# Sample state products by head, on four row groups of TensorE in two rounds of four

## The reference, cut to what matters

```python
b_last = b[:, :, -1:, :]
S_new = jnp.exp(b_last[:, :, 0, :, None]) * S + jnp.einsum(
    'bhsk,bhsv->bhkv', kc * jnp.exp(b_last - b), vc)
```

## Time and profile before

| what | value |
|---|---|
| median of 3 runs | 2166.18 us (2164.0 to 2167.3) |
| the profiled execution, its own time | 2165.37 us |
| its span, first to last instruction | 2163.8 us |
| mean granted TensorE clock | 0.972 |
| PE busy (matmul) | 2046.5 us, 95% |
| DVE busy | 1569.3 us, 73% |
| ACT busy | 1287.0 us, 59% |
| POOL busy | 769.2 us, 36% |

### The profile page before, as it was taken

The page is one execution under the profiler, slowest core; times in us unless marked ns, Lnnn a source line. Parts: engine busy times, 40 slices in busy tenths (PEclk is TensorE's granted clock), DMA queues, the critical chain, the costliest instruction groups (busy, mean ns, idle before and its releaser), DMA issues.

```text
span 2163.8 us, 38715 instructions
## 1 busy us (share of the span) xinstructions
PE 2046.5 (95%) x11913; PEld 1499.0 (69%) x11947; DVE 1569.3 (73%) x2132; ACT 1287.0 (59%) x1717; POOL 769.2 (36%) x997
## 2 busy tenths in 40 slices
PE   6998999999968999999999999999999999999994
PEld 4896676666646676676676668877676677788562
DVE  4533456666668687787786769988797798898657
ACT  3532344333416676676775667867676786888554
POOL 3225345555723232222242223432243243334124
PEclk8999999999968999999999999999999999999997
DMA  9767611121367788898887779999899899999765
GB/s 348 231 226 256 189 50 49 52 70 46 97 221 296 275 315 291 290 338 310 294 306 243 281 270 382 390 339 365 288 366 347 289 349 333 366 370 392 258 221 182
DMA packets 154531, 572.26 MB, mean 264 GB/s; under 512 B 22560, under 2 KB 41773, under 8 KB 120165
## 3 DMA queue, kind: packets, MB, share of 16 engines
q1 hardware_dynamic: 127405, 511.87, 62.7%
q0 software_dynamic: 25520, 56.53, 10.5%
q10 hardware_dynamic: 1552, 3.13, 0.4%
HBM read 521.36 MB, written 50.29 MB: 264 GB/s over the span
## 4 chain that ended last, share of the span: by engine, by line
PE 58%; issue 4%; ACT 4%; DVE 3%; ACTq 0%; DVEq 0%; DMA 0%; POOLq 0%
PE pg L2242 9%; PE pg L2243 9%; PE pg L2245 9%; PE py L2201 6%; PE py L2177 6%; PE py L2178 5%; PE py L2181 5%; PE pg L2215 3%; ACT hi L2378 3%; PE pt L2172 1%; PE pt L2166 1%; DVE lo L2475 1%; PE pg L2235 1%; PE pt L2187 0%; ACT L2398 0%
## 5 line engine op out<-in xcount | busy, mean ns | idle before, releaser
L2242 PE MATMUL pg<-hi,xs 128*128 128x512 f32 x1056 | 432.9, 410 | 0.0
L2243 PE MATMUL pg<-lo,xs 128*128 128x512 f32 x1056 | 412.5, 391 | 0.0
L2475 DVE TENSOR_TENSOR lo<-spare,hi 128x1024 fp32r<-128x1024 f32 x264 | 306.3, 1221 | 81.5 <-ACT hi L2378 78.6
L2475 DVE TENSOR_TENSOR lo<-w_out,hi 128x1024 fp32r<-128x1024 f32 x272 | 313.8, 1220 | 70.4 <-ACT hi L2378 69.3
L2245 PE MATMUL pg<-hi,xs 128*128 128x512 f32 x1056 | 326.1, 390 | 0.0
L2475 DVE TENSOR_TENSOR lo<-raw,hi 128x1024 fp32r<-128x1024 f32 x264 | 314.0, 1220 | 7.1
L2378 ACT ACTIVATE hi<-w_out 128x1024 fp32r<-128x1024 f32 x272 | 265.5, 1049 | 34.6 <-SPq L2009 27.2
L2378 ACT ACTIVATE hi<-spare 128x1024 fp32r<-128x1024 f32 x264 | 259.2, 1048 | 43.2 <-PE pg L2245 43.2
L2378 ACT ACTIVATE hi<-raw 128x1024 fp32r<-128x1024 f32 x264 | 270.4, 1056 | 23.3 <-PE pg L2245 23.3
L2242 PEld LDWEIGHTS pg<-hi,xs 128*128 128x128 f32 x1056 | 198.5, 188 | 71.6 <-issue 14.1
L2245 PEld LDWEIGHTS pg<-hi,xs 128*128 128x128 f32 x1056 | 198.5, 188 | 42.5
(11 more groups left out here) (486 smaller groups left out, 3571.2 us busy)
## 6 DMA issues: line engine op xcount, KB each, us to landing
w_out<-in_w_gu SPq DMA_DIRECT2D x136, 1024.0 KB, 6.9
spare<-in_w_gu SPq DMA_DIRECT2D x132, 1024.0 KB, 10.2
raw<-in_w_down SPq DMA_DIRECT2D x132, 1024.0 KB
ada_w<-in_w_ada SPq DMA_DIRECT2D x4, 2048.0 KB
spare<-in_w_ada SPq DMA_DIRECT2D x4, 2048.0 KB
moe_rows<-small SPq DMA_DIRECT2D x9, 512.0 KB, 7.0
w_v<-in_w_in SPq DMA_DIRECT2D x2, 2048.0 KB, 17.2
w_i<-in_w_in SPq DMA_DIRECT2D x2, 2048.0 KB
```

The costliest lines, as they stand in the source:

```text
L2242: pe.matmul(pg[u][b][:, :], xs[:, kt, 0, :], wh[:, u, :], start=False, stop=False)
L2243: pe.matmul(pg[u][b][:, :], xs[:, kt, 0, :], wl[:, u, :], start=False, stop=False)
L2475: dve.tensor_tensor(lo[q % RING][:, :, :], grain(q % GRAINS), hi[q % RING][:, :, :].bitcast(F32), ALU.subtract).then_inc(s["lo"], 1)
```

## The change

The same products are laid out by head. The keys of the four heads stand in four groups of 32 partitions (`kT` is now 128 x 128), and so do the values (`v4`, and `Vz` with all heads, 128 partitions by 128 values for each sequence). A matmul takes the 32 rows of one head and streams four sequences at once (512 columns), into a bank of its own: X1, X2, X0 and L0 for the heads 0 to 3. There are two rounds of four matmuls. VectorE adds by head and half of the sequences, eight adds of 128 x 4 x 128. The keys reach their place by four matmuls with the identity (`columns_k_sample`) where there were four transposes, ScalarE copies the values once more (into `v4`), and VectorE copies the sequence mask into the three other groups near the program's start.

```diff
         sample = {**quarters(1, 0, ("f", "q", "k", "lf")), **quarters(1, 1, ("b", "eb", "dk", "kend")),
-                  **quarters(1, 2, ("lev0", "lev1", "A", "wd")), **quarters(1, 7, ("row0",)),
-                  "v": strip(1, 3), "gs": strip(1, 4), "o": strip(1, 5), "kT": strip(1, 6), "mixT": w_v[:, 7, 0:KT * NS],
+                  **quarters(1, 2, ("lev0", "lev1", "A", "wd")), **quarters(1, 7, ("row0", "v4")),
+                  "v": strip(1, 3), "gs": strip(1, 4), "o": strip(1, 5), "kT": strip(1, 6)[:, 0:P], "mixT": w_v[:, 7, 0:KT * NS],
...
-        Vz = w_g[0:NS, :, :]
+        Vz = w_g[:, 0:2, :].rearrange("p a (b v) -> p (a b) v", v=P)
...
-        state_ps = (X1, X2, X0, X1, X2, X0, X1, X2)
+        state_ps = (X1, X2, X0, L0)
+        ROUND = NB // 2
...
             for j in range(NB):
-                sp.wait_ge(s["S_s"], j + 1)
+                sp.wait_ge(s["S_s"], (j // ROUND + 1) * H)
                 sp.dma_start(out["S_s"][0, j].rearrange("h k v -> k h v"), S0[:, j, :, :]).then_inc(s["st_out"], 16)
...
-            def states_sample(t, first, end):
-                pe.wait_ge(s["kT"], t + 1)
-                pe.wait_ge(s["Vz"], 1)
-                for j in range(first, end):
-                    bank = state_ps[j]
-                    if j >= 3:
-                        pe.wait_ge(s["S_s"], j - 2)
-                    for m in range(H):
-                        last = pe.matmul(bank[:, m * P:(m + 1) * P], sample["kT"][0:NS, m * P:(m + 1) * P], Vz[:, j, m * P:(m + 1) * P], start=True, stop=True)
-                    last.then_inc(s["S_s_mm"], 1)
+            def columns_k_sample(t):
+                pe.wait_ge(s["kend"], t + 1)
+                for m in range(H):
+                    last = pe.matmul(X3[m * NS:(m + 1) * NS, 0:P], sample["kend"][:, m * NS:(m + 1) * NS], ident[:, :], start=True, stop=True)
+                last.then_inc(s["kT_ps"], 1)
+
+            def states_sample(t, half):
+                if half == 0:
+                    pe.wait_ge(s["kT"], t + 1)
+                    pe.wait_ge(s["Vz"], 1)
+                    pe.wait_ge(s["vrow"], 2)
+                    pe.wait_ge(s["x1"], TILES + 1)
+                else:
+                    pe.wait_ge(s["S_s"], H)
+                for m in range(H):
+                    rows_m = slice(m * NS, (m + 1) * NS)
+                    last = pe.matmul(state_ps[m][:, :], sample["kT"][rows_m, :], Vz[rows_m, half * ROUND:(half + 1) * ROUND, :], start=True, stop=True)
+                last.then_inc(s["S_s_mm"], 1)
...
-            transpose_k(u, NS, X3)
+            columns_k_sample(u)
...
-            states_sample(u, 0, 1)
             pe.wait_ge(s["lg"], t)
             route_rows(t, P)
-            pe.wait_ge(s["vrow"], 2)
-            states_sample(u, 1, 3)
+            states_sample(u, 0)
             route_logits(t, P)
             pe.wait_ge(s["lg"], u)
             route_rows(u, NS)
             pe.wait_ge(s["rank_used"], t)
             rank(t, P, X3)
             route_logits(u, NS)
-            states_sample(u, 3, 5)
             pe.wait_ge(s["rank_used"], u)
             rank(u, NS, X3)
-            states_sample(u, 5, NB)
+            states_sample(u, 1)
...
                 act.wait_ge(s["sam_mm"], 2)
+                act.activation(sample["v4"], X3[:, 0:P], ACT.Copy)
...
-                act.activation(of(T)["kT"][0:T, :], bank[0:T, :], ACT.Copy).then_inc(s["kT"], 1)
+                act.activation(of(T)["kT"][:, :], bank[:, :] if T == P else bank[:, 0:P], ACT.Copy).then_inc(s["kT"], 1)
...
-            def add_state(j):
-                dve.wait_ge(s["S_dec"], j + 1)
-                dve.wait_ge(s["S_s_mm"], j + 1)
-                rows = S0[:, j, :, :].rearrange("p h v -> p (h v)")
-                dve.tensor_tensor(rows, rows, state_ps[j][:, :], ALU.add).then_inc(s["S_s"], 1)
+            def add_state(half, m):
+                js = slice(half * ROUND, (half + 1) * ROUND)
+                dve.wait_ge(s["S_dec"], (half + 1) * ROUND)
+                dve.wait_ge(s["S_s_mm"], half + 1)
+                dve.tensor_tensor(S0[:, js, m, :], S0[:, js, m, :], state_ps[m][:, :].rearrange("p (j v) -> p j v", j=ROUND), ALU.add).then_inc(s["S_s"], 1)
...
+            for m in range(1, H):
+                dve.tensor_copy(seqmask[m * NS:(m + 1) * NS, :], seqmask[0:NS, :])
...
-            add_state(0)
+            add_state(0, 0)
             logits(t, P)
             choose(t, P)
             h2_high(u, T)
-            add_state(1)
+            add_state(0, 1)
             weigh(t, P)
             place(t, P, X3)
-            add_state(2)
+            add_state(0, 2)
             logits(u, T)
             choose(u, T)
-            for j in range(3, 6):
-                add_state(j)
+            add_state(0, 3)
             weigh(u, T)
             place(u, T, X3)
-            for j in range(6, NB):
-                add_state(j)
+            for m in range(H):
+                add_state(1, m)
...
+            pool.wait_ge(s["S"], 1)
             for j in range(NB):
-                last = pool.tensor_scalar(Vz[:, j, :], sample["v"][0:NS, :], seqmask[:, j:j + 1], 0.0, ALU.mult, ALU.add)
+                last = pool.tensor_scalar(Vz[:, j, :], sample["v4"], seqmask[:, j:j + 1], 0.0, ALU.mult, ALU.add)
```

More of the change, by code:

```diff
@@ L136, in mixing @@
         reset_s = sb("reset_s", [P, H * NS])
-        seqmask = sb("seqmask", [NS, NB])
+        seqmask = sb("seqmask", [P, NB])
         iota_e = sb("iota_e", [P, E])
@@ L1739, in _ @@
             pool.memset(reset_s[:, :], 1.0)
-            pool.memset(seqmask[:, :], 1.0)
+            pool.memset(seqmask[0:NS, :], 1.0)
             for m in masks:
@@ L1747, in _ @@
             pool.memset(reset_s[:, :].rearrange("p (g t) -> p g t", t=TS)[:, :, 0:1], 0.0)
-            pool.affine_select(out=seqmask[:, :], in_=seqmask[:, :], compare_op=ALU.is_ge, fill=0.0,
+            pool.affine_select(out=seqmask[0:NS, :], in_=seqmask[0:NS, :], compare_op=ALU.is_ge, fill=0.0,
                                base=0, pattern=[[-TS, NB]], channel_multiplier=1).then_inc(s["c0"], 1)
             pool.wait_ge(s["c0"], 5)
-            pool.affine_select(out=seqmask[:, :], in_=seqmask[:, :], compare_op=ALU.is_ge, fill=0.0,
+            pool.affine_select(out=seqmask[0:NS, :], in_=seqmask[0:NS, :], compare_op=ALU.is_ge, fill=0.0,
                                base=TS - 1, pattern=[[TS, NB]], channel_multiplier=-1)
```

## The result

The changed kernel took 2173.2 us (median of 8 runs, 2168.9 to 2175.3), the kernel before 2165.2 (8 runs, 2163.2 to 2167.3) in the same session: a ratio of 1.0035, 95% interval 1.0026 to 1.0044. That is 8 us slower, where 2166.0 and no measurable change were forecast, and outside the range.

A forecast was written before the change was run, and what follows sets the result against it. Bound: the barrier between `mixing` and `experts`, three arrivals within 1.0 us. Savings of 3.0 (listing) and 1.8 us (last add) end ahead of weights 0.6 later; barrier -0.2 on median 2166.18 gives 2166.0 us, range 2162.5 to 2170.0.

The forecast's parts named there:

- behind which everything starts anew: Barrier between `mixing` and `experts`: the change lies before it, so the barrier's line by instruction was read first.
- Rival 4: Clock or experts part shifts for reasons of its own, either sign, by up to 3.3 us; chance 0.07.
- Rounds: TensorE's four-matmul rounds: row groups run at once, 1.1 to 1.6 us, or 2.1 to 2.7 at the lower clock.
- Rival 3: TensorE's row groups don't run at once: second round 7.2 us, total 2171.0 to 2175.1 us; chance 0.07.
- First round: TensorE between tile 7's transposes and router logits: runs from 612.6 to 613.7 or 614.2, costing nothing.
- Logits: Tile 7's router logits behind the first round: end by 616.9, or 617.9 if the clock falls earlier, not holding VectorE.
- GpSimd's drain: Ahead of the barrier: starts 3.0 us earlier with the listing, over by 647.5 if it keeps its 7 us.
- rival 2: GpSimd's drain hangs on DMA traffic, not the listing: +0.6 to +0.8 us, 2166.8 to 2167.0; chance 0.18.
- Stores: Four state stores go out together at 633.05; weights behind them start 0.6 us later, bounds -0.5 and +0.8.
- the 0.6 of the sum: SyncE's end ahead of the barrier: 649.5 + 0.6 = 650.1 us, from weights going out later.
- the forecast of -0.2: The barrier opens at some 650.4 instead of 650.6 us; chance of the forecast 0.55.
- The 5.1 us for a first round one by one at the lower clock: Loss if the first round's row groups run one after the other at the lower clock; 1.0 at full clock.

The follow-up runs named there:

- e2: The kernel before with 166 idle TensorE instructions behind its last state product: 2176.9 us, 1.0053 of the kernel before.
- e1: The changed kernel with 90 idle TensorE instructions behind its last state product: 2165.2 us, 1.0005 of the kernel before.
- e3: The changed kernel with 45 idle TensorE instructions behind its last state product: 2167.1 us, 1.0006 of the kernel before.
- e4: The changed kernel with 135 idle TensorE instructions behind its last state product: 2165.4 us, 0.9999 of the kernel before.
- e5: The changed kernel with 90 never-run TensorE instructions between the jump and its target: 2167.0 us, 1.0002 of the kernel before.
- e6: The kernel before with 166 never-run TensorE instructions between the jump and its target: 2167.3 us, 1.0003 of the kernel before.
- e9: The changed kernel with one idle TensorE instruction behind its last state product: 2166.5 us, 1.0006 of the kernel before.
- e7: The changed kernel loading only a quarter of each weight chunk from the second item on: 2163.0 us, 0.9991 of the kernel before.
- e8: The changed kernel with quarter weight loads from the second item on and 90 idle TensorE instructions: 2159.0 us, 0.9965 of the kernel before.
- e10: The changed kernel with 236 never-run TensorE instructions between the jump and its target: 2279.4 us, 1.0524 of the kernel before.
- e11: The changed kernel with TensorE's first experts transposes placed behind the items' loop in code but run before it: 2172.8 us, 1.0038 of the kernel before.
- e12: The changed kernel with the first transposes placed behind the items' loop, run before it, plus 90 idle instructions: 2169.8 us, 1.0020 of the kernel before.

## Why the prediction was wrong

**The step that failed** is in its first paragraph: the change lies before the barrier, "behind which everything starts anew". Time starts anew there; the code does not. Each instruction taken out of `mixing` moves all that TensorE runs later. Rival 4 named the place, "the experts part shifts for reasons of their own", with no mechanism, and priced it at the spread of three runs, 3.3 us. Its price is one more piece: 5.75 us at the first stop, 0.8 at the second; with the 1.15 ahead of them and a rest that makes the profiled spans' 8.1. How the 0.8 comes about wasn't tried: at the second item the stop is 5.51 us here and 6.38 in e2, and 3.95 to 4.92 in the kernel before, e1, e3, e4, e5, e6 and e9.

**The change itself** did what was forecast for it. With its code moved by 1, 45, 90 or 135 instructions, or the target alone by 91, it stands at 0.9999 to 1.0006 of the kernel before, every interval within 0.2% of one. Point by point:

- Rounds: 2.1 us (613.11 to 615.20), and 2.2 for the second (628.5 to 630.7), the second inside its 2.1 to 2.7. Rival 3 is refuted.
- First round: forecast for the full clock, 1.1 to 1.6 us. In this profile it took 2.1: the granted clock fell to 0.50, the lower of its two levels, at 611.8, ahead of the round, with TensorE idle for 2.38 us in the wait for bank L0. Logits end at 618.75 instead of 617.9 at the latest and hold VectorE for 0.60 us, which the prediction named as something that would make it wrong. The other traces of the new layout are milder. In e3, e4, e5, e7, e8 and e10, after the same idle time, the clock falls only behind the round, which takes 1.14 us, and nothing is held. In e1, e9, e11 and e12 it falls within the round: 1.5 to 1.6 us, and VectorE is held for 0.14 at most. The profiled execution passed its delay on: `slotc_s` is 0.8 us behind its forecast (631.5 for 630.7), and so is the last add (633.9 for 633.05).
- GpSimd's drain over by 647.5, as forecast: its start moved 3.0 us with the listing, against rival 2.
- Stores: single times say little, since one execution comes to the tail some 3 us later than another (601.4 to 604.7). So count from the end of the out projection, in all eleven traces of the new layout, against the kernel before and e6. The weights go out 31.8 to 32.5 us after it, 31.9 before: 0.1 us earlier to 0.6 later, inside the bounds. SyncE is through after 46.1 to 47.2, the median 46.6, against 46.0 and 45.9: the 0.6 of the sum. But it lies in the transfers, not in their start: the median is 31.8 for the start, and from there to SyncE's end it is 14.8 instead of 14.1 and 14.0. SyncE is the last of the three in all eleven. The barrier opens after 46.4 to 47.5, the median 46.9, against 47.1 and 47.2. That agrees with the forecast of -0.2, in a spread of 1.1 us, so some tenths are not shown.
- The 5.1 us for a first round one by one at the lower clock does not follow from the rows named (612.6 + 7.2 + 2.7 is 4.6 behind 617.9, and 5.6 with the further microsecond). Nothing hung on it.

**What the profile of before had to say.** The rows that the prediction rests on stop at the barrier, but for one of the earlier trace rows. The jump of 6.16 us and the stop of 3.76 stood in the same trace, but the timeline puts the stop down to VectorE's `lo`, which looks like data. It is not: the subtraction this row waits for, the first item's 21st, ended at 686.46, 11 us before. And in all fourteen traces TensorE starts again at the first item's stop 1.4 to 1.7 us behind the end of a packet of code (695.08 + 1.02 in the kernel before, start at 697.80; 702.51 + 1.08 in the changed one, start at 704.97). A rival was to be had from this: `foot` has 51 instructions as built and a piece 256, so after any change of length the chance is about 0.2 that an edge falls inside it. By e10 and e12, where 20 and 25 instructions cover 4.2 and 5.1 us, only an edge within some 28 instructions of the target costs anything: an estimated chance of 0.1, at a price of up to one more fetch, 6 us. The range should have reached to it.

## What to carry to other kernels

An edit that changes the number of instructions moves all code behind it, and where a loop first jumps over code that wasn't run yet, one place more or less can cost several microseconds, here more than the edit itself. So before a small loss or gain is put down to an edit, add idle instructions that restore the old length, and look at the sequencer's branches that last microseconds instead of 0.2. Where a stop's named releaser is a semaphore long raised, look at the instruction queue.

## What was not expected of the hardware

- The first item's branch to code not held took 6.1 to 6.6 us under full DMA traffic and 3.6 to 3.9 under light, for a packet that itself moves in about 1 us. The waiting is most of it.
- With a loop of 1,548 TensorE instructions the whole run fetched 37 pieces, three of them late (1129 to 1166 us) and without a stop; with one of 1,618 it fetched 119 and took 5% longer. The Trainium skill (the same page and section) gives TensorE room for 2,048, which would be eight pieces. By the edges that e9 shows, e10's loop touches eight and e6's seven, so eight seem not to have fitted. That is one run each, and a full item runs code in only some of them; what is kept, and how long, stays open.
- Three pieces came before the loop in e11, by their place in the code the one with the jump's target among them, and the jump still fetched one: 652.78 us for the first of the three, 699.98 for that one. In the kernel before, the second item's jump to the same target takes 6.0 us once more, and leaves TensorE idle for 4.71.
